# Keys' rotary part in the first layers: tokens as moving operand in four column groups, the partial sums added and turned by one product

## The reference

```python
h = _rmsnorm(h_res, ln1_g[layer])            # 272 tokens (16 meta + 256) x 1024
proj = h @ w_in[layer]
(c_q, c_kv, k_rope, sb_q, sb_k, sb_v,
 df_q, df_k, df_v, gate_logits) = _split_cols(proj, IN_SIZES)
q = _heads(_rmsnorm(c_q, mla_cq_norm_g[layer]) @ mla_w_uq[layer], MLA_HEADS)
kv = _heads(_rmsnorm(c_kv, mla_ckv_norm_g[layer]) @ mla_w_ukv[layer], MLA_HEADS)
k_nope, v_mla = kv[..., :MLA_NOPE], kv[..., MLA_NOPE:]
k_r = jnp.broadcast_to(k_rope[:, None], (b, MLA_HEADS, p_len, MLA_ROPE))
k = jnp.concatenate([k_nope, k_r], axis=-1)
q = _rmsnorm(q, mla_q_norm_g[layer]); k = _rmsnorm(k, mla_k_norm_g[layer])
```

## Time and profile before

| | us |
|---|---|
| timed, median of 3 | 2589.15 (2588.43 to 2592.13) |
| the profiled execution | 2594.4 |
| its span, first to last instruction | 2593.1 |
| PE busy in the span | 2523.5 (97%) |
| DVE, ACT, POOL busy | 1102.9, 506.7, 277.3 |

### The profile page before, as it was taken

One profiled execution on the slowest core, in us unless ns is written; L12 is line 12 of the kernel. 1 busy time (PEld: TensorE's weight loads), 2 busy tenths in 40 slices (PEclk: granted clock), 3 DMA queues, 4 the chain that ended last, 5 costly groups with the idle time before them and its releaser, 6 DMA issues.

```text
span 2593.1 us, 50004 instructions
## 1 busy us (share of the span) xinstructions
PE 2523.5 (97%) x21294; PEld 1976.6 (76%) x21294; DVE 1102.9 (43%) x2368; ACT 506.7 (20%) x1110; POOL 277.3 (11%) x213
## 2 busy tenths in 40 slices
PE   9999999999999999999999999999999899999998
PEld 6787789997788899988866666665888766666665
DVE  4546448875455378853321111112674321111112
ACT  2323312102333122011210111111342210111102
POOL 0000016630000046410000000000000000000000
PEclk9999999999999999999899999999999999999999
DMA  5223346763233466755389999996331589999995
GB/s 201 95 98 114 114 180 259 293 255 122 95 112 115 145 269 254 310 201 221 145 335 380 390 420 419 419 420 277 116 114 51 227 349 375 400 420 419 419 420 206
DMA packets 96028, 659.58 MB, mean 254 GB/s; under 512 B 12878, under 2 KB 14430, under 8 KB 17728
## 3 DMA queue, kind: packets, MB, share of 16 engines
q1 hardware_dynamic: 90736, 647.28, 62.8%
q0 software_dynamic: 4784, 8.80, 1.0%
q10 hardware_dynamic: 288, 0.31, 0.0%
HBM read 660.92 MB, written 4.19 MB: 256 GB/s over the span
## 4 chain that ended last, share of the span: by engine, by line
PE 89%; DVE 3%; DMA 3%; POOL 2%; ACT 2%; issue 1%; SPq 0%; DVEq 0%; POOLq 0%; ACTq 0%
PE PS L600 85%; PE PS L605 4%; ACT AR L2613 1%; DMA AR<-in_experts 1%; DMA wmoe<-in_experts 1%; DMA wdense<-in_experts 1%; DVE wmoe L1712 1%; DVE wmoe L1912 1%; POOL AR L3181 1%; DVE wmoe L1914 1%; DMA wdense<-in_dense 0%; POOL AR L3179 0%; POOL wmoe L3170 0%; POOL AR L3182 0%; POOL wmoe L3184 0%
## 5 line engine op out<-in xcount | busy, mean ns | idle before, releaser
L600 PE MATMUL PS<-H,wdense 128*128 128x256 f32 (+4 forms) x2432 | 515.3, 368 | 6.4 <-ACT H L2613 2.2
L600 PE MATMUL PS<-AR 128*128 128x128 f32 (+12 forms) x4848 | 498.7, 312 | 14.9 <-ACT AR L2613 10.0
L600 PEld LDWEIGHTS PS<-H,wdense 128*128 128x128 f32 (+1 forms) x2432 | 422.7, 192 | 75.2 <-issue 10.6
L600 PEld LDWEIGHTS PS<-AR 128*32 128x32 f32 (+5 forms) x4848 | 353.2, 148 | 134.7 <-issue 71.5
L2613 ACT ACTIVATE AR<-PS 128x256 f32<-128x256 f32 (+11 forms) x433 | 185.6, 437 | 1343.5 <-PE PS L600 999.4
L600 PE MATMUL PS<-wmoe,AR 128*32 128x256 f32 (+4 forms) x3280 | 343.7, 413 | 5.8 <-DMA wmoe<-in_experts 5.6
L600 PE MATMUL PS<-AR,wdense 128*128 128x256 f32 (+3 forms) x1472 | 283.6, 348 | 2.2 <-DVE AR L2359 2.2
L600 PE MATMUL PS<-AR,CST 128*128 128x256 f32 (+3 forms) x1096 | 271.6, 387 | 12.8 <-ACT AR L2613 12.8
L600 PEld LDWEIGHTS PS<-AR,wdense 128*128 128x128 f32 x1472 | 243.9, 191 | 33.1 <-DVE AR L2359 3.1
L600 PE MATMUL PS<-wdense,AR 128*32 128x256 f32 (+7 forms) x2112 | 257.0, 420 | 1.8 <-DMA wdense<-in_experts 1.3
L600 PEld LDWEIGHTS PS<-wmoe,AR 128*32 128x32 f32 (+2 forms) x3280 | 166.0, 119 | 116.4 <-issue 51.8
(11 more groups left out here) (318 smaller groups left out, 2049.1 us busy)
## 6 DMA issues: line engine op xcount, KB each, us to landing
wmoe<-in_experts SPq DMA_DIRECT2D x180, 1024.0 KB, 17.1
wdense<-in_dense SPq DMA_DIRECT2D x172, 1024.0 KB, 4.8
wdense<-in_experts SPq DMA_DIRECT2D x114, 1024.0 KB, 17.7
AR<-in_experts SPq DMA_DIRECT2D x90, 1024.0 KB, 17.1
wmoe<-in_ada SPq DMA_DIRECT2D x48, 1024.0 KB, 8.4
AR<-in_dense SPq DMA_DIRECT2D x4, 1024.0 KB, 7.5
tokens<-AR POOLq DMA_DIRECT2D x4, 512.0 KB, 4.0
wdense<-in_dense SPq DMA_DIRECT2D x2, 768.0 KB, 9.3
```

Source lines behind the costliest of these rows:

```text
L600: return te.matmul(out, lhsT, rhs, start=start, stop=stop, skip_group_check=True)
```

## The change

The weights of the rotary part become the stationary operand (32 columns), and all 272 tokens move. Slice k of the eight goes to column group k % 4, so two slices are summed in each group, and four partial sums stand under each other on 128 partitions. ACT copies them to `WORK`. After `uq`, PE multiplies them (stationary, three tiles of tokens) with `STACKED`, four 32 x 32 identities under each other, made once by DVE at the start: this adds the four partial sums and turns the result to tokens on partitions, in a bank of its own. DVE's copies to `KR` move behind the last copies of `ukv`, with an `own()` before and after them. The loads are the same.

```diff
@@ tensor_program, first_layer
-            o = bank(("k_rope", L), VE)
-            for t, (t0, n) in enumerate(TILES):
-                m = sum_k(o[0:n, 32 * t:32 * t + 32], [H[:, k, t0:t0 + n] for k in range(DC)],
-                          [slot[:, k, P:P + 32] for k in range(DC)])
-            PE.up(m, "k_rope", L)
+            o = bank(("k_rope parts", L), AC)
+            for k in range(DC):
+                g = k % 4
+                m = mm(o[32 * g:32 * g + 32, 0:T], slot[:, k, P:P + 32], H[:, k, :], start=k < 4, stop=k > 3)
+            PE.up(m, "k_rope parts", L)
             used()
...
             used()
+            o = bank(("k_rope", L), VE)
+            te.wait_ge(VE.sem, VE.of("stacked"))
+            te.wait_ge(AC.sem, AC.of("k_rope parts", L))
+            for t, (t0, n) in enumerate(TILES):
+                m = mm(o[0:n, 32 * t:32 * t + 32], WORK[:, 3 * T + t0:3 * T + t0 + n], STACKED[:, :])
+            PE.up(m, "k_rope", L)
             slot = take(1, 1024)
@@ vector_program, first_layer
             VE.up(ve.memset(KR, 0.0))
-            own()
-            ve.wait_ge(PE.sem, PE.of("k_rope", L))
-            for t, (t0, n) in enumerate(TILES):
-                VE.up(ve.tensor_copy(KR[0:n, t, :], ps("k_rope", L)[0:n, 32 * t:32 * t + 32]))
-            VE.mark("k_rope", L)
...
+            ve.wait_ge(PE.sem, PE.of("k_rope", L))
+            own()
+            for t, (t0, n) in enumerate(TILES):
+                VE.up(ve.tensor_copy(KR[0:n, t, :], ps("k_rope", L)[0:n, 32 * t:32 * t + 32]))
+            VE.mark("k_rope", L)
+            own()
             VE.up(ve.tensor_copy(KTM[:, :, :, 64:96], KR.unsqueeze(2).broadcast_to([P, 3, 8, 32])), "k whole", L)
@@ vector_program, start
         ve.wait_ge(ones_load, 16)
+        VE.up(ve.tensor_tensor(STACKED[:], ident[:, 0:ROPE], ident[:, ROPE:2 * ROPE], ALU.add))
+        for j in (2, 3):
+            own()
+            VE.up(ve.tensor_tensor(STACKED[:], STACKED[:], ident[:, j * ROPE:(j + 1) * ROPE], ALU.add), "stacked")
@@ scalar_program, first_layer
             AC.up(act(WORK[:, 0:2 * T]...), "cq squared", L, 0)
+            copy(("k_rope parts", L), WORK[:, 3 * T:4 * T], ps("k_rope parts", L)[:, 0:T])
```

More of the change, by code:

```diff
@@ L302, in build @@
     ST = sb("ST", [P, 512], F32)
-    EPSC = sb("EPSC", [P, 4], F32)
+    EPSC, STACKED = sb("EPSC", [P, 4], F32), sb("STACKED", [P, ROPE], F32)
     ARENA_N = 19608
```

## The result

| | before | after |
|---|---|---|
| timed, median, us (7 runs each) | 2589.15 | 2575.45 (2569.59 to 2581.5) |
| ratio, 95% interval | | 0.9947 (0.9932 to 0.9961) |
| its profiled span, us | 2593.1 | 2568.3 |

The change makes the kernel faster by 13.7 us; I had said 6.0 and a range that ended at 9. Executions of one kernel differ by 10 us and more, so medians and intervals are compared. In two further sets of runs the ratio was 0.9929 (0.991 to 0.9948) and 0.9933 (0.9921 to 0.9945). The profiled execution after is the fastest of its seven, that of before was above its median, so the 24.8 us between the two spans overstate the gain.

What follows compares the result with a forecast made beforehand. PE, busy for 97% of the span, was taken as the bound. Each layer gained 3.50 us, together 7.0; counting three quarters of the clock's 3.6 left 6.0, so 2589.15 became 2583.1 us, range 2580.0 to 2588.0.

Steps and rivals of the forecast that it cites:

- Step 1, 2 and 4: PE at `k_rope`, layer 0: products removed 4.44 us, parts added 1.15, clock restored 1.48; layer 1: 4.37, 1.15, 1.55.
- Step 3: PE, each layer: three added products from `STACKED` that sum and turn the parts cost 0.73 us.
- Step 5: DVE, each layer: copies to `KR` ahead of `k whole` delay `roped q`, so PE stands 0.54 us longer.
- From the profile to the timed runs: Whole kernel: three quarters of the clock's 3.6 us counted, so 3.4 + 2.6 = 6.0 us gained when timed.
- Step 6: `STACKED`'s three DVE additions, one more bank per layer and earlier slot release cost nothing; additions 0.7 us once if uncovered.
- I count no loss there: Behind layer 1: long transfers in the chain should move earlier with PE, so none of the gain is lost.
- A: Timed executions mostly lack the two clock falls at `k_rope`; only 3.4 us gained, 2585.7 us; chance 0.28.
- B: The parts' column groups don't overlap or idle between sets; 2.5 us a layer lost, 2588 us; chance 0.05.
- C: The gain is given back later at a wait for experts' weights; 2589 us, no change; chance 0.06.
- D: Longer wait at the queries' turning lowers the clock in transposes behind; 1.5 to 1.7 us a fall, 2592.5; chance 0.04.

Runs made afterwards that it cites:

- one_group: The changed kernel with all eight products of the parts in one column group, summed in PSUM; 2577.59 us, ratio 0.9958 to the kernel before.
- after_again: The changed kernel run once more with no further edit; 2572.11 us, ratio 0.9933 to the kernel before.
- clock_kept: The kernel before with the first `sb qk` moved between the second and third tile of `k_rope`; 2583.73 us, ratio 0.9976.
- code_as_before: The changed kernel with 102 more instructions, waits on a long-reached semaphore, ahead of PE's first product; 2586.81 us, ratio 0.9982 to the kernel before.

## Why the prediction was wrong

*Step 1, 2 and 4 (what goes, the parts, the clock)* were right. I had 4.44 - 1.15 + 1.48 = 4.77 us for the stretch of layer 0; it is 13.35 - 8.59 = 4.76. The parts alone are 8.59 - 3.76 - 3.67 = 1.16 us, with `cq` 2 and `sb qk` as in the earlier trace rows, for 1.15 said. In layer 1 the first `sb qk` sums come 605.76 - 597.68 = 8.08 us earlier, 3.39 of them from layer 0, so 4.69, for 4.77.

*Step 3 (sum and turn)*: 0.73 said, 0.72 measured.

*Step 5 (late copies)*: 0.54 said; 0.61 in layer 0. In layer 1 the turning waits just as long, but PE's next wait, for ACT, is 0.54 us shorter (1.10 to 0.56), so there it costs about 0.1. That is why 7.26 us are gained behind layer 1 and not 7.0.

*From the profile to the timed runs.* 6.0 said; 6.8 by the medians and 8.7 by the ratio (5.3 to 12.1) measured with the waits' price taken off. Three quarters for the clock was fair: 11 of 14 openings show the fall.

*Step 6, "without cost", failed, and with it "I count no loss there".* I priced `STACKED` by the three additions that fill it, and the new code by its running time. Neither the tile's 128 bytes nor the number of instructions was in the sum, and these two gave 8 to 10 us of 15 to 17: the tile moved the destinations of the experts' transfers to multiples of 256 bytes (5 to 7 us by the last comparison, 3 to 10 by all), and the 102 missing instructions moved a fetch of code out of a transfer that POOL, DVE and PE wait for one after the other (3.3 us in time; in the profile 1.67 of wait, and 1.55 of clock behind it where the clock falls, in five profiles of eight). I had looked at transfers only for whether they start later, and asked only about a loss.

*The rivals.* A did not come: most openings before have the fall, and the direct part is 6.8 us or more, with an interval that leaves 3.4 out. B is refuted by the 8.59 us themselves, beside the 11.31 of `one_group`, C by the profiles, in which the 7.15 us gained at 1000 us are 24.8 at the end. D, a fall of the clock at the turning of the queries, did come once, in `after_again`, where a window from 62.6 to 66.0 us shows

```profile
62.60:66.00 3.40, 3.40 (x13) 2.32 (x13) 2.76 (x2) 1.88 (x8) 0.00 (x0) 0.50 0.33 137
```

in one of 20 openings. This fall is 6.8 us long, another of 3.4 us comes right behind the keys' turning, at 86.5, and at 100 us the profile stands 5.5 us behind the one after, so D's 1.5 to 1.7 us a fall were too little for such a pair. Right behind the keys' turning lie also the falls at 84.5 in `clock_kept` and at 94.1 in `code_as_before`. The mechanism exists, but rarely.

*What stays open:* why the clock falls behind the pause of 1.90 us in some profiles and not in others; how much of the addresses' 3 to 10 us goes through PE's waits for weights, since those are 8.4 us before and 2.4 to 4.7 after without the timed gain following them closely; whether the tile's 128 bytes, which move `AR` for the engines as well, do anything there but through the loads; and whether other fetches of code weigh on transfers elsewhere, since every edit moves all of them.

## What to carry to other kernels

A change has sizes beside its work: the bytes of a new tile move every tile behind it, and its instruction count moves every fetch of code behind it. Before a gain or loss of a few tenths of a per cent is credited to an edit, run the kernel before with a tile of the same size, and the change with its tile allocated last. Where large loads saturate the DMA engines, look at where in a partition the tile begins, since it is free to choose.

## What the runs showed of the hardware

- Large loads into slots that begin at a multiple of 256 bytes of a partition ran at 424 to 426 GB/s where they saturate the DMA engines, and at 418 to 420 when the slots began 128 or 192 bytes past one.
- One fetch of PE's code (16 KB) takes one of the 16 DMA engines for about 1.0 us. In the stretch of a transfer it made POOL's wait for the landing 1.0 to 1.5 us longer, and PE's at the end of the chain by 0.5 or 1.7. The Trainium skill ("Runtime: NRT & Kernel Launch", "Instruction fetch mechanics") calls the cost of these blocks mostly hidden; the cost seen here is that of the transfer beside them, which was late.
- An instruction in PE's queue that only waits, on a semaphore that has long been reached, takes 0.1 us (5.6 us for 52).
- The same DVE addition over 128x512 took 0.68 us when it started ahead of one of POOL's, by 0.01 us in `code_as_before`, and 1.45 to 1.79 when it started 0.03 to 0.37 us behind it.
